# Last expert: sum rows read back to the core, its output added by 0/1 products on TensorE, final squares shared with ScalarE

## What is computed

```python
def moe_swiglu(h, router_w, w_gate, w_up, w_down):
    ...
    for e in range(N_EXPERTS):
        out = out + combine[..., e:e + 1] * swiglu(h, w_gate[e], w_up[e], w_down[e])
    return out
...
            h = h + moe_swiglu(hn, router_w[i], moe_w_gate[i], moe_w_up[i], moe_w_down[i])
...
    y = rms_norm(h, final_norm_g)
```

## Time and profile before

| what | us |
|---|---|
| three runs without a profile | 1644.64, 1647.79, 1649.31; median 1647.79 |
| the profiled execution | 1648.3 |
| its span, first to last instruction | 1646.6 |
| last matmul ends (from the span's start) | 1620.7 |

### The profile page before, as it was taken

One profiled execution on the slowest core, in us unless ns is written; L12 is line 12 of the kernel. 1 busy time (PEld: TensorE's weight loads), 2 busy tenths in 40 slices (PEclk: granted clock), 3 DMA queues, 4 the chain that ended last, 5 costly groups with the idle time before them and its releaser, 6 DMA issues.

```text
span 1646.6 us, 25254 instructions
## 1 busy us (share of the span) xinstructions
PE 1566.2 (95%) x8782; PEld 1387.3 (84%) x8783; DVE 1173.3 (71%) x1497; ACT 1000.4 (61%) x1184; POOL 110.6 (7%) x112
## 2 busy tenths in 40 slices
PE   6989999999999998999969999999999999999993
PEld 5889999899999878999858888888888888888882
DVE  6677437544444477734738989898998989898894
ACT  5663324443433575233437787878888787887772
POOL 3020120000000002111000000000000000010000
PEclk9999999999999999999979999999999999999997
DMA  7434453455445332444449999999999999999994
GB/s 221 133 118 128 136 154 117 127 152 145 146 142 159 116 116 93 136 140 128 141 135 352 359 373 372 374 375 366 374 369 372 379 373 369 368 377 366 373 367 155
DMA packets 223037, 399.08 MB, mean 242 GB/s; under 512 B 12336, under 2 KB 103520, under 8 KB 222960
## 3 DMA queue, kind: packets, MB, share of 16 engines
q1 hardware_dynamic: 215920, 372.84, 64.9%
q0 software_dynamic: 6544, 23.37, 5.2%
q10 hardware_dynamic: 496, 1.84, 0.3%
HBM read 383.84 MB, written 14.16 MB: 242 GB/s over the span
## 4 chain that ended last, share of the span: by engine, by line
PE 72%; DVE 9%; ACT 6%; DMA 6%; issue 6%; ACTq 0%; SPq 0%; DVEq 0%; POOLq 0%; POOL 0%
PE bank L1462 10%; PE bank L1464 10%; PE bank L1463 10%; PE bank L1774 7%; PE bank L1776 7%; PE bank L1775 6%; PE bank L1766 4%; PE bank L1765 4%; PE bank L1767 4%; DMA weights_raw<-in_moe_w_up 3%; DVE weights_low L1348 3%; DMA weights_raw<-in_moe_w_down 2%; PE bank L1608 2%; ACT weights_high L909 2%; ACT weights_high L689 2%
## 5 line engine op out<-in xcount | busy, mean ns | idle before, releaser
L1348 DVE TENSOR_TENSOR weights_low<-weights_raw,weights_high 128x1024 fp32r<-128x1024 f32 x522 | 621.4, 1220 | 76.6 <-ACT weights_high L909 65.3
L909 ACT ACTIVATE weights_high<-weights_raw 128x1024 fp32r<-128x1024 f32 x522 | 548.8, 1060 | 144.4 <-DMA weights_raw<-in_moe_w_up 56.4
L972 DVE TENSOR_TENSOR weights_low<-weights_raw,weights_high 128x1024 fp32r<-128x1024 f32 (+1 forms) x186 | 225.2, 1216 | 297.4 <-ACT weights_high L689 297.3
L689 ACT ACTIVATE weights_high<-weights_raw 128x1024 fp32r<-128x1024 f32 (+1 forms) x186 | 193.4, 1045 | 246.6 <-PE bank L1464 236.3
L1462 PE MATMUL bank<-moving_high,weights_high 128*128 128x320 f32 x944 | 299.7, 317 | 1.0 <-DVE moving_low L1043 1.0
L1463 PE MATMUL bank<-moving_low,weights_high 128*128 128x320 f32 x944 | 295.5, 313 | 0.0
L1464 PE MATMUL bank<-moving_high,weights_low 128*128 128x320 f32 x944 | 295.4, 313 | 0.0
L1774 PE MATMUL bank<-weights_high,expert_in_high 128*128 128x512 f32 (+1 forms) x768 | 290.6, 378 | 1.7 <-DVE weights_low L1348 0.8
L1776 PE MATMUL bank<-weights_high,expert_in_low 128*128 128x512 f32 (+1 forms) x768 | 286.6, 373 | 0.0
L1775 PE MATMUL bank<-weights_low,expert_in_high 128*128 128x512 f32 (+1 forms) x768 | 286.4, 373 | 0.0
L1462 PEld LDWEIGHTS bank<-moving_high,weights_high 128*128 128x128 f32 x944 | 181.3, 192 | 4.6 <-issue 1.9
(11 more groups left out here) (298 smaller groups left out, 1813.9 us busy)
## 6 DMA issues: line engine op xcount, KB each, us to landing
weights_raw<-in_moe_w_gate SPq DMA_DIRECT2D x176, 512.0 KB, 5.5
weights_raw<-in_moe_w_up SPq DMA_DIRECT2D x176, 512.0 KB, 5.7
weights_raw<-in_moe_w_down SPq DMA_DIRECT2D x176, 512.0 KB, 5.3
weights_raw<-in_w_in SPq DMA_DIRECT2D x80, 512.0 KB, 3.6
weights_raw<-in_dense_w_gate SPq DMA_DIRECT2D x22, 512.0 KB, 3.8
weights_raw<-in_dense_w_up SPq DMA_DIRECT2D x22, 512.0 KB, 3.7
weights_raw<-in_w_out SPq DMA_DIRECT2D x16, 512.0 KB, 3.4
weights_raw<-in_dense_w_down SPq DMA_DIRECT2D x16, 512.0 KB, 3.4
```

The source lines that it names most:

```text
L689: fn(whi[:, p % RING, 0:n], raw[:, p % RING, 0:n], ACT.Copy).then_inc(high_done, 1)
L909: fn(whi[:, p % RING, 0:n], raw[:, p % RING, 0:n], ACT.Copy).then_inc(high_done, 1)
L1348: v.tensor_tensor(wlo[:, p % RING, 0:n], raw[:, p % RING, 0:n], whi[:, p % RING, 0:n].bitcast(F), ALU.subtract).then_inc(low_done, 1)
```

## The change

In the last expert (the written-out one) and at the end:

- POOL issues the three DMAs from `SUM` into `acc` as soon as the scatter of the seventh expert has landed, while the last expert's weights stream. The last expert's scatter is gone.
- After down chunk 5, PE turns `pick` (three transposes into bank 0). ACT loads the table of Sqrt there and copies the turned matrix to `pick_t`.
- After the down products ACT writes `yh`, the high part of output times gate, in two halves; the first half waits only for bank 6. DVE writes the low part `yl` from PSUM. PE multiplies `pick_t` by both: twelve matmuls of 512 columns into banks 0 to 5. DVE adds the six results to `acc`. The flag of the spare blocks is read and jumped by DVE after these adds, and by PE after these products.
- A small memset by DVE releases the last norm. DVE squares tile 0; ACT squares tiles 1 and 2. The tiles are finished in the order 1, 0, 2.

```diff
+        for item in range(NE - 1):
+            pool.wait_ge(idx_ready, item + 2)
+            gather()
             pool.wait_ge(y_added, 16 * (NKEEP + item))
             pool.wait_ge(y_ready, NO + 2 * item + 2)
             scatter_add()
-        pool.wait_ge(y_added, 16 * (NKEEP + NE))
-        extra_blocks(pool, extra)
+        pool.wait_ge(y_added, 16 * (NKEEP + NE - 1))
         for t, (t0, sz) in enumerate(TOK):
             pool.dma_start(acc[0:sz, t, :], SUM[t0:t0 + sz]).then_inc(acc_in[t], 16)
+        extra_blocks(pool, extra)
...
+            if kind == "down" and j == PICK_AT and not ahead:
+                nc.scalar.preload_act_table(ACT.Sqrt)
...
+                act.wait_ge(pickt_psum, item - (NE - 2))
+                fn(pick_t[:], bank[0][:, 0:T], ACT.Copy).then_inc(pickt_ready, 1)
+            if i == NEC - 1 and not ahead:
+                act.wait_ge(kept, item + 1)
+                for hh in range(2):
...
+                    fn(yh[:, 512 * hh:512 * hh + 512], bank[DOWN_BANK + hh][:], ACT.Copy, scale=gate_s[:, 0:1]).then_inc(
+                        y_ready, 1)
...
+        act.wait_ge(sums_final, 1)
+        for t in ENDS:
+            sz = TOK[t][1]
+            if t:
+                link(fn(He[0:sz, D:2 * D], acc[0:sz, t], ACT.Square, accum_out=ssf[0:sz, t:t + 1]))
...
+        def rows_back(item):
+            for hh in range(2):
+                hs = slice(512 * hh, 512 * hh + 512)
+                dve.wait_ge(y_ready, 2 * item + (NO + hh + 1))
+                v.scalar_tensor_tensor(out=yl[:, hs], in0=bank[DOWN_BANK + hh][:], scalar=gate_s[:, 0:1],
+                                       in1=yh[:, hs].bitcast(F), op0=ALU.mult, op1=ALU.subtract).then_inc(yl_ready, 1)
+            for n, (t, hf_) in enumerate(BACK):
...
+                dve.wait_ge(back_psum, NO * item - NO * (NE - 1) + (n + 1))
+                v.tensor_tensor(acc[0:sz, t, hs], acc[0:sz, t, hs], bank[n][0:sz, :], ALU.add).then_inc(back_added, 1)
...
+            if kind == "down" and j == PICK_AT and not ahead:
+                pe.wait_ge(he_ready, NG * item + (NG - 1))
+                for t, (t0, sz) in enumerate(TOK):
+                    ins = nc.tensor.transpose(bank[0][:, t0:t0 + sz], pick[0:sz, t, :], ident[0:sz, 0:sz])
+                ins.then_inc(pickt_psum, 1)
+            if i == NEC - 1 and not ahead:
+                pe.wait_ge(pickt_ready, item - (NE - 2))
+                for n, (t, hf_) in enumerate(BACK):
...
+                    pe.wait_ge(yl_ready, 2 * item - 2 * (NE - 1) + (hf_ + 1))
+                    mm(bank[n][0:sz, :], pick_t[:, t0:t0 + sz], yh[:, hs], start=True, stop=False)
+                    ins = mm(bank[n][0:sz, :], pick_t[:, t0:t0 + sz], yl[:, hs], start=False, stop=True)
+                    ins.then_inc(back_psum, 1)
```

More of the change, by code:

```diff
@@ L257, in hybrid_trunk_program @@
     assert o <= nc.sbuf_usable_end
+    pick_t = later("pick_turned", [128, T], R, region + 4 * NT * D)
+    yh = later("last_out_high", [128, D], R, region + 4 * NT * D + 4 * T)
+    yl = later("last_out_low", [128, D], R, region + 4 * NT * D + 4 * T + 4 * D)
+    assert 4 * T + 8 * D <= 4 * NT * D
     xeh = later("expert_in_high", [128, KD, CAP], R, xh_at)
@@ L406, in hybrid_trunk_program @@
     y_added = sem("expert_out_added")
+    half_down = sem("expert_out_first_half_psum")
+    pickt_psum = sem("pick_turned_psum")
+    pickt_ready = sem("pick_turned_ready")
+    yl_ready = sem("last_out_low_ready")
+    back_psum = sem("rows_back_psum")
+    back_added = sem("rows_back_added")
+    sums_final = sem("sum_rows_final")
     acc_in = [sem(f"sum_rows_in_{t}") for t in range(NT)]
@@ L423, in hybrid_trunk_program @@
     NKEEP = 3
+    PICK_AT = 5
+    BACK = [(t, hf_) for hf_ in range(2) for t in range(NT)]
+    ENDS = [1, 0, 2]
     ROW_BANK = [0, 1, 2, 3, 5, 6]
@@ L517, in _ @@
         extra_blocks(sp, lambda item, n: load_expert(item, n % NE))
-        for t in range(NT):
-            sp.wait_ge(fout_ready, t + 1)
+        for n, t in enumerate(ENDS):
+            sp.wait_ge(fout_ready, n + 1)
             if t < PAIRS:
@@ L930, in chunk @@
                 expert_in_high(item + 1)
-            if i == NEC - 1:
+            if kind == "down" and j == PICK_AT and not ahead:
+                nc.scalar.preload_act_table(ACT.Sqrt)
+                if not isinstance(item, int):
+                    act.wait_ge(back_psum, NO * item - NO * (NE - 1))
+                act.wait_ge(pickt_psum, item - (NE - 2))
[3 more added lines that the diff above has]
+                for hh in range(2):
+                    if hh == 0:
+                        act.wait_ge(half_down, item + 1)
+                    else:
+                        act.wait_ge(pe_mark, 2 * NEC * item + (MB + 2 * NEC))
+                    fn(yh[:, 512 * hh:512 * hh + 512], bank[DOWN_BANK + hh][:], ACT.Copy, scale=gate_s[:, 0:1]).then_inc(
+                        y_ready, 1)
+            if i == NEC - 1 and ahead:
                 act.wait_ge(pe_mark, 2 * NEC * item + (MB + 2 * NEC))
@@ L952, in _ @@
         extra_blocks(act, extra)
-        for t, (_, sz) in enumerate(TOK):
-            act.wait_ge(fsq_ready, t + 1)
+        act.wait_ge(sums_final, 1)
[3 more added lines that the diff above has]
+                link(fn(He[0:sz, D:2 * D], acc[0:sz, t], ACT.Square, accum_out=ssf[0:sz, t:t + 1]))
+            else:
+                act.wait_ge(fsq_ready, 1)
             fn(rf[0:sz, t:t + 1], ssf[0:sz, t:t + 1], ACT.Sqrt, bias=eps_t[0:sz], scale=1.0 / D).then_inc(froot_ready, 1)
@@ L1321, in rows_of_slots, with keep_rows @@
             v.tensor_tensor(idx[:], bank[DOWN_BANK][:, 0:1], own_row[:], ALU.add).then_inc(idx_ready, 1)
-        def keep_rows(item):
+        def keep_rows(item, ahead):
             dve.wait_ge(idx_ready, item + 1)
-            dve.wait_ge(y_added, 16 * item + 16 * NKEEP)
+            dve.wait_ge(y_added, 16 * item + 16 * NKEEP if ahead else 16 * (NE - 1 + NKEEP))
             v.tensor_copy(gate_s[:], gate[:])
@@ L1367, in chunk @@
                 if j == KEEP_AT:
-                    keep_rows(item)
+                    keep_rows(item, ahead)
                 if j == CHOOSE_AT and ahead:
@@ L1414, in _ @@
                             chunk(item, i, NEC, False)
-                        dve.wait_ge(y_ready, 2 * item + (NO + 2))
+                        dve.wait_ge(back_added, NO * item - NO * (NE - 2))
                         v.memset(cgate[:], 0.0)
         dve.wait_ge(gfin_in, 16)
[L1419 to L1430, removed]
+        dve.wait_ge(back_added, NO)
+        v.memset(ssf[:], 0.0).then_inc(sums_final, 1)
+        dve.wait_ge(sums_final, 1)
+        v.tensor_tensor_reduce(out=He[:, 0:D], in0=acc[:, 0], in1=acc[:, 0], scale=1.0, scalar=0.0, op0=ALU.mult,
+                               op1=ALU.add, accum_out=ssf[:, 0:1]).then_inc(fsq_ready, 1)
+        for n, t in enumerate(ENDS):
+            sz = TOK[t][1]
+            dve.wait_ge(froot_ready, n + 1)
             link(v.reciprocal(rf[0:sz, t:t + 1], rf[0:sz, t:t + 1]))
@@ L1768, in chunk @@
                                      stop=kk == KF - 1)
+                            if kk == KF - 1 and hh == 0:
+                                ins.then_inc(half_down, 1)
                     else:
@@ L1786, in chunk @@
                 expert_rows_turned(item + 1)
+            if kind == "down" and j == PICK_AT and not ahead:
[3 more added lines that the diff above has]
+                ins.then_inc(pickt_psum, 1)
+            if i == NEC - 1 and not ahead:
+                pe.wait_ge(pickt_ready, item - (NE - 2))
+                for n, (t, hf_) in enumerate(BACK):
+                    t0, sz = TOK[t]
+                    hs = slice(512 * hf_, 512 * hf_ + 512)
+                    pe.wait_ge(yl_ready, 2 * item - 2 * (NE - 1) + (hf_ + 1))
+                    mm(bank[n][0:sz, :], pick_t[:, t0:t0 + sz], yh[:, hs], start=True, stop=False)
+                    ins = mm(bank[n][0:sz, :], pick_t[:, t0:t0 + sz], yl[:, hs], start=False, stop=True)
+                    ins.then_inc(back_psum, 1)
         def extra(item, n):
```

13 lines of the change are left out of this document (4 added, 9 removed).

## The result

| kernel | median us | ratio to the kernel before, 95% interval |
|---|---|---|
| before | 1650.66 (20 runs) | |
| changed | 1643.59 (20 runs) | 0.9962 (0.9948 to 0.9976) |
| changed, measured once more (chip 2) | 1642.01 (6 runs; before 1652.09) | 0.9942 (0.9929 to 0.9955) |

The changed kernel is faster, by 6.3 us by the first ratio (0.0038 x 1650.66) and 9.6 by the second. The profiled execution has a span of 1639.5 us instead of 1646.6. Of that difference of 7.1 us, 1.3 is no work of the change: the last expert's first piece happened to start 1.3 us earlier in this execution (1525.4 instead of 1526.7). In the profiles of this record, with the same code up to that point in nearly all, this start lies anywhere between 1525.4 and 1536.0.

A forecast was written before the change was run, and what follows sets the result against it. PE (95% busy) and the DMA engines were taken as near their limits in the expert stage, with a serial tail behind. Terms -10.8 + 2.9 + 0.3 = -7.6 us gave 1640.7 profiled, 1640.2 median; range 1637.0 to 1645.0.

The forecast's parts named there:

- rival A: Last expert: the early load costs per byte as the scatter did, 6.2 us instead of 2.9, giving 1643.5; chance 0.15.
- steps 1 to 9: Tail from T, the last down matmul's end, to the span's end: 15.1 us instead of 25.9, gain 10.8.
- The six adds: Tail, on DVE: 0.68 us each with some overlap, 3.8 us in all, from T+1.45 to T+5.25.
- The flag and the jump: Tail, DVE reading the spare blocks' flag and jumping after the adds: 0.5 us, range 0 to 1.5.
- The row sum of ACT's square: Tail, ACT's square of 128x1024: its row sum adds between 0 and 0.4 us, taken as 0.15.
- The early load: Last expert: 1.31 MB on full DMA engines takes 3.1 us, less 0.2 lead; PE stands 2.9 longer, range 1.9 to 6.2.
- The transposes: Last expert, PE turning `pick`: three transposes on the path, nothing hides them, 0.3 us.
- ACT at chunk 5: Last expert: table load and copy, 1.7 us ahead of a high part, covered by 0.4 us; cost 0, up to 0.7.
- B: Last expert: the early load is hidden beside the weights, PE's stand under 1 us, giving 1638.0; chance 0.08.
- C: Tail: a second table load of 1.28 us, with slower flag and jump +2.3, giving 1642.5; chance 0.11.
- D: PE's clock falls to half while waiting for weights: +2.7 us, 1650.5; slower from 15.2 us at half clock; chance 0.04.
- E: Tail: the end does not change as written, half of the gain is left, giving 1645; chance 0.04.

The follow-up runs named there:

- experiment 2: Changed kernel with two more loads of 512 KB each behind the three early ones; no time given, PE's wait 7.8 us instead of 5.4.
- experiments 6 and 7: Changed kernel with the early load cut into 2 KB rows (six DMAs), or issued by SP between weight pieces; no times given, PE's wait 3.6 and 4.5 us.

## Why the prediction was right

The time came out inside the range, with the sign and the two opposed parts as forecast: a shorter tail, and a longer last expert because the load delays the weights. Part of the closeness is luck. In the profiled pair the span fell by 7.1 us, near the forecast of 7.6, but 1.3 of that is the earlier start; without it the change is worth 5.8. The measured terms, 10.9 less 4.4 less 0.6, give 5.9. And the median of 1643.59, read against the forecast's 1640.2, looks like rival A's 1643.5. That is chance: the kernel before came out at 1650.66 over 20 runs instead of the 1647.79 from which the forecast was counted. By its steps:

**The tail (steps 1 to 9).** Forecast 15.1 us, measured 14.95. The second half of the relay started 0.4 late: the first product starts at T+1.0 instead of T+0.8, and the adds at T+1.8 instead of T+1.45. The six adds took 3.67 (forecast 3.8). The flag and the jump cost 0.2 instead of 0.5, as the flag is read beside the adds. The row sum of ACT's square is 0.19 (forecast 0.15). The rest agrees within 0.1.

**The early load.** This is the term that was too small: 2.9 forecast, 4.4 measured in the profiled pair, and 3.6 to 3.8 in the mean of all profiles by the two measures. The mechanism was right (no lead and full engines; that nothing gives it back is not shown by the times). The weak step is "I take 3.1, because its rows of 4 KB are plain reads": it priced all 1.31 MB alike, while the 64-row tile costs an estimated 1.5 to 1.7 us for 0.26 MB. Per byte, the 128-row tiles are near the forecast (2.3 us per MB in experiment 2).

**The transposes.** 0.3 forecast, 0.6 measured. The rate of a run of eight does not hold for three: eight took 0.79 us and three took 0.52.

**ACT at chunk 5.** Forecast at 0 and measured at 0. The copy starts 1.29 us after the table load's beginning; the drain of 1380 ns that the Trainium skill (ScalarE: Activation LUTs, What ACT_TABLE_LOAD costs) states does not show here. Had it been there, the lead of 1.35 us would have just been used up.

**The rivals.** A's price (6.2) lies above the 4.4 of the pair, and above every early load of 1.31 MB measured; per byte the 128-row tiles do not cost what the scatter did, though the measured size lies between A and the forecast. B falls with PE's wait. C falls: no table load stands in the tail. D did not happen in the changed kernel's two profiles. Its mechanism is real: in two of the runs with an early load (experiments 6 and 7) the clock was at the lower level for some 3.4 us while PE multiplied, at most 1.7 us of products each, where D needed 15.2 us to turn the result. How often it happens in runs without a profile is not known. E falls with six adds that wait for nothing but PE.

## What to carry to other kernels

In a stage where the DMA engines are full, moving a transfer into it saves its latency at the end and pays its bytes at once; read the lead of the consumer first, and look for the place where the stream has ended but the consumer has not, which is where a transfer is free. Spreading it inside the stage does not help if the stream cannot catch up. Do not price a transfer by its bytes alone: here the tile of 64 rows cost more than one of 128.

## What the runs showed of the hardware

While the load of 64 rows of 4 KB runs beside the weights, the full DMA engines together move 216 to 255 GB/s, on POOL's queue (224, 250, 255) and on SP's (216) alike. Beside the loads of 128 rows they move 393 to 408. Why was not tried: it was always the same 64 rows of `SUM`, so the number of rows is not told apart from their place in HBM. Against weight packets of 2 KB, a load with packets of 4 KB took two thirds of the bytes moved (1.03 of 1.61 MB). In two executions in which PE stood for 1.9 and 3.6 us behind the load, the granted clock was at 0.50 for some 3.4 us with work at hand; after stands of 1.2 and 1.5 us in the changed kernel, and of 2.1 and 2.5 in experiment 2, it stayed at 1.00.
